# A fused two-block kernel: the opening's norm sums moved to TensorE and its order rewritten

## What is computed

```python
def rms_norm(x, w):
    y = x * lax.rsqrt(jnp.mean(x * x, axis=-1, keepdims=True) + EPS)
    return y * w
def modulate(x, norm_w, shift, scale):
    return rms_norm(x, norm_w) * (1 + scale) + shift

mod_l = silu(c) @ ada_w[0] + ada_b[0]       # six vectors of 1024; the same for ctx with c_ctx
hl = modulate(x,   norm_mix_w[0], sh1,  sc1)
hc = modulate(ctx, norm_mix_w[0], csh1, csc1)
pl, pc = hl @ w_in, hc @ w_in
```

## Time and profile before

| | |
|---|---|
| three executions, median | 2278.91 us (2278.24 to 2280.76) |
| profiled execution, its own time | 2280.79 us |
| its span in the profile | 2278.8 us |
| TensorE busy (matmuls) | 2218.6 us, 97% of the span |
| VectorE, ScalarE, GpSimd busy | 52%, 39%, 41% |
| mean granted clock of TensorE | 0.993 of full |

### The profile page before, as it was taken

One profiled execution on the slowest core, in us unless ns is written; L12 is line 12 of the kernel. 1 busy time (PEld: TensorE's weight loads), 2 busy tenths in 40 slices (PEclk: granted clock), 3 DMA queues, 4 the chain that ended last, 5 costly groups with the idle time before them and its releaser, 6 DMA issues.

```text
span 2278.8 us, 36911 instructions
## 1 busy us (share of the span) xinstructions
PE 2218.6 (97%) x13959; PEld 1904.4 (84%) x13959; DVE 1177.3 (52%) x1926; ACT 879.6 (39%) x1532; POOL 935.8 (41%) x767
## 2 busy tenths in 40 slices
PE   6999999999999999999999999999999999999998
PEld 4878979888888888888899988888888887788777
DVE  5784781657777763335244365553334115762273
ACT  5434343341111113325455442223444236742572
POOL 2435453343343333325343155554665441154313
PEclk9999999999999999999999999999999999999999
DMA  7242241125555541111211025553223232123212
GB/s 281 77 149 75 73 160 61 56 93 194 193 193 189 189 147 59 61 65 65 76 43 33 10 93 190 188 184 120 92 94 107 93 101 75 49 84 94 78 48 74
DMA packets 67720, 245.40 MB, mean 108 GB/s; under 512 B 7376, under 2 KB 11728, under 8 KB 66960
## 3 DMA queue, kind: packets, MB, share of 16 engines
q1 hardware_dynamic: 67360, 242.94, 31.4%
q0 software_dynamic: 240, 0.79, 0.1%
HBM read 240.81 MB, written 2.10 MB: 107 GB/s over the span
## 4 chain that ended last, share of the span: by engine, by line
PE 78%; DVE 7%; issue 7%; POOL 4%; ACT 3%; DMA 0%; POOLq 0%; DVEq 0%; SPq 0%; ACTq 0%
PE ps L887 14%; PE ps L888 14%; PE ps L889 14%; PE ps L1779 4%; PE ps L1781 4%; PE ps L1782 4%; POOL w_low L489 4%; PE ps L924 2%; PE ps L926 2%; PE ps L925 2%; PE ps L2009 2%; PE ps L1995 2%; PE ps L636 2%; PE ps L1947 1%; DVE arena L3005 1%
## 5 line engine op out<-in xcount | busy, mean ns | idle before, releaser
L489 POOL TENSOR_TENSOR w_low<-ring,w_high 128x512 fp32r<-128x512 f32 (+2 forms) x534 | 747.5, 1422 | 1048.1 <-ACT w_high L480 1048.1
L480 ACT ACTIVATE w_high<-ring 128x1024 fp32r<-128x1024 f32 (+2 forms) x267 | 275.1, 1031 | 928.4 <-PE ps L889 620.6
L887 PE MATMUL ps<-h_high,w_high 128*128 128x512 f32 x1040 | 408.7, 393 | 8.4 <-DVE h_low L736 5.5
L888 PE MATMUL ps<-h_low,w_high 128*128 128x512 f32 x1040 | 406.0, 390 | 0.0
L889 PE MATMUL ps<-h_high,w_low 128*128 128x512 f32 x1040 | 405.4, 390 | 0.0
L887 PEld LDWEIGHTS ps<-h_high,w_high 128*128 128x128 f32 x1040 | 195.8, 188 | 55.8 <-DVE h_low L736 6.0
L889 PEld LDWEIGHTS ps<-h_high,w_low 128*128 128x128 f32 x1040 | 195.6, 188 | 41.5
L888 PEld LDWEIGHTS ps<-h_low,w_high 128*128 128x128 f32 x1040 | 195.7, 188 | 37.8
L3240 DVE TENSOR_TENSOR hidden<-arena,hidden 128x1536 fp32r<-128x1536 f32 (+1 forms) x42 | 87.2, 2077 | 193.3 <-ACT hidden L2362 193.3
L1779 PE MATMUL ps<-hidden,w_high 128*128 128x512 f32 (+1 forms) x504 | 178.6, 354 | 0.0
L2907 DVE CUSTOM_DVE_ANT_0 const<-const,arena 128x1024 f32<-128x1024 f32 x96 | 149.0, 1566 | 57.2 <-DMA const<-late_w_dram 57.1
(11 more groups left out here) (553 smaller groups left out, 4766.6 us busy)
## 6 DMA issues: line engine op xcount, KB each, us to landing
const<-late_w_dram SPq DMA_DIRECT2D x112, 512.0 KB, 5.0
ring<-up_dram SPq DMA_DIRECT2D x88, 512.0 KB, 3.2
ring<-down_dram SPq DMA_DIRECT2D x44, 512.0 KB, 3.2
XB<-ada_dram SPq DMA_DIRECT2D x22, 768.0 KB, 5.5
ring<-winE_dram SPq DMA_DIRECT2D x32, 512.0 KB, 3.5
ring<-win_dram SPq DMA_DIRECT2D x20, 512.0 KB, 3.2
ring<-winC_dram SPq DMA_DIRECT2D x20, 512.0 KB, 3.5
arena<-ada_dram SPq DMA_DIRECT2D x10, 768.0 KB, 19.8
```

What stands on the lines that cost most here:

```text
L480: nc.scalar.activation(WH[p][:, 0:L], RAW[p][:, 0:L], ACT.Copy).then_inc(w_hi, 1)
L489: ins = nc.gpsimd.tensor_tensor(WL[p][:, to], RAW[p][:, to], WH[p][:, to].bitcast(F32), ALU.subtract)
L887: nc.tensor.matmul(bank[:, 0:n], wh[:, cols], hi, start=(k == 0), stop=False)
L888: nc.tensor.matmul(bank[:, 0:n], wh[:, cols], lo, start=False, stop=False)
```

## The change

- The load of the latents is cut in two halves of four tiles. The load of the context goes behind both pieces of group 2's `ada_w` (the sixth piece).
- The squares of the opening are no longer added on VectorE: each is written to its own place (in the buffer that later holds the scaled tile), and TensorE sums all eight tiles of a sequence itself, so that `mean` takes 64 passes for the latents and 32 for the context.
- Latents and context have a root, an inverse and a bank each. The context's squares, mean, root and spread move behind latent tile 3.
- TensorE's new order: mean of the latents, group sums 0, spread of the latents, turn 0, group sums 1, turn 1, tile 0, group sums 2, turn 2, tiles 1, 2, 3, mean of the context, group sums 3, spread of the context, turn 3, group sums 4, tile 4, turn 4, group sums 5, tile 5, turn 5, tiles 6 and 7.
- ScalarE's row copies go behind the high parts of the tiles ahead of them; in `hgrn`, `split_hi` of a chunk goes before the wait for the context sums of the same turn instead of behind their exponential.

The core of the diff:

```diff
-    adaT=(FIRST_MODS, (4,)), n0=(3, (1, 5, 6)), ...
+    adaT=(FIRST_MODS, (4,)), n0=(4, (1, 5, 6, 3)), ...
-ADDED = ("n0", "n1", "n3", "n5", "n6")
+ADDED = ("n1", "n3", "n5", "n6")
-BATCHED = dict(n0=(range(2),), ro0=(range(4),), ...
+BATCHED = dict(ro0=(range(4),), ...
         def square_at(stage, k, j):
+            if stage == "n0":
+                return H[k][:, j, :]
...
-            sp.dma_start(XL, dram["xl"]).then_inc(x_first, 16)
-            sp.dma_start(XC, dram["xc"]).then_inc(x_in, 16)
+            for x in range(2):
+                some = slice(KT // 2 * x, KT // 2 * (x + 1))
+                sp.dma_start(XL[:, some, :], dram["xl"][:, some, :]).then_inc(x_first[x], 16)
             for u in range(2 * FIRST_MODS):
...
+                if u == 5:
+                    sp.dma_start(XC, dram["xc"]).then_inc(x_in, 16)
...
+            mean(pe, "n0", 0)
             mod_sums(0)
-            for k in range(2):
-                mean(pe, "n0", k)
+            spread(pe, "n0", 0)
             mod_turn(0)
-            spread(pe, "n0", 0)
             mod_sums(1)
+            mod_turn(1)
+            first_latent(0)
+            mod_sums(2)
+            mod_turn(2)
+            first_latent(1)
+            first_latent(2)
+            first_latent(3)
+            mean(pe, "n0", 1)
+            mod_sums(3)
             spread(pe, "n0", 1)
-            mod_turn(1)
-            mod_sums(2)
-            first_latent(0)
-            mod_turn(2)
-            mod_sums(3)
-            first_latent(1)
             mod_turn(3)
-            first_latent(2)
             mod_sums(4)
-            first_latent(3)
+            first_latent(4)
             mod_turn(4)
-            first_latent(4)
             mod_sums(5)
...
-            for j in range(KT):
-                square("n0", 0, j)
-            act.wait_ge(x_in, 16)
-            for j in range(KT):
-                square("n0", 1, j)
+            for x in range(2):
+                act.wait_ge(x_first[x], 16)
+                for j in range(KT // 2 * x, KT // 2 * (x + 1)):
+                    square("n0", 0, j)
+            root("n0", 0)
             mod_row(0)
             for k in range(2):
                 split_hi("win0", k)
-            root("n0", 0)
+            shift_high("n0", 0, (0,))
             mod_row(1)
-            shift_high("n0", 0, (0,))
+            shift_high("n0", 0, (1,))
             mod_row(2)
-            shift_high("n0", 0, (1,))
+            shift_high("n0", 0, (2,))
+            act.wait_ge(x_in, 16)
+            for j in range(KT // 2):
+                square("n0", 1, j)
+            shift_high("n0", 0, (3,))
+            for j in range(KT // 2, KT):
+                square("n0", 1, j)
+            root("n0", 1)
             mod_row(3)
-            shift_high("n0", 0, (2, 3))
+            shift_high("n0", 0, (4,))
             mod_row(4)
-            shift_high("n0", 0, (4, 5))
+            shift_high("n0", 0, (5,))
             mod_row(5)
...
+                    if i and not (r and c < 2):
+                        split_hi(win, c + 2)
                     bank = await_sums(act, win, g)
                     taken(A(A_b[d][:, j, a:a + n], bank[:, 0:n], ACT.Exp, scale=-1.0), win, g)
-                    if i and not (r and c < 2):
-                        split_hi(win, c + 2)
...
-            for k, j in squared("n0"):
-                if j:
-                    add_square("n0", k, j)
             invert("n0", 0)
             first_columns(0)
...
             scale_tile("n0", 0, 3)
+            invert("n0", 1)
             first_columns(3)
```

More of the change, by code:

```diff
@@ L114 @@
 SUMS = dict(
-    adaT=(FIRST_MODS, (4,)), n0=(3, (1, 5, 6)), win0=(19, B5), hgS0=(6 * SCORE_SUMS, (0, 1, 2, 3)), hgK0=(6 + ROUND_MODS[0], (5,)), hgU0=(12, (4, 6)), ro0=(5, (5, 6)),
+    adaT=(FIRST_MODS, (4,)), n0=(4, (1, 5, 6, 3)), win0=(19, B5), hgS0=(6 * SCORE_SUMS, (0, 1, 2, 3)), hgK0=(6 + ROUND_MODS[0], (5,)), hgU0=(12, (4, 6)), ro0=(5, (5, 6)),
     win1=(19, B5), hgS1=(6 * SCORE_SUMS, (0, 1, 2, 3)), hgK1=(6 + ROUND_MODS[1], (5,)), hgU1=(12, (4, 6)), ro1=(5, (5, 6)),
@@ L156 @@
 NORM_STAGES = [x for x in SUMS if x in ("n0", "ro0", "ro1", "n1", "n2", "nlat", "nqk", "n3", "n4", "n5", "n6")]
-ADDED = ("n0", "n1", "n3", "n5", "n6")
-LAST_APART = ADDED[1:]
+ADDED = ("n1", "n3", "n5", "n6")
 PAIRED = (("n2", 0), ("n4", 0))
-BATCHED = dict(n0=(range(2),), ro0=(range(4),), ro1=(range(4),), nlat=(range(1), range(1, 5)), nqk=(range(9),))
+BATCHED = dict(ro0=(range(4),), ro1=(range(4),), nlat=(range(1), range(1, 5)), nqk=(range(9),))
 RS_COLS = 48
@@ L370, in two_blocks @@
         late_c, late_silu = sem("late_c"), sem("late_silu")
-        x_in, x_first = sem("x_in"), sem("x_first")
+        x_in, x_first = sem("x_in"), [sem(f"x_first{x}") for x in range(2)]
         raw_full, raw_spent, down_spent = ([sem(f"{x}{p}") for p in range(2)] for x in ("raw_full", "raw_spent", "down_spent"))
@@ L506, in squared @@
                 last = 2 if stage == "n6" else 0
-                if stage == "n0":
-                    return [(k, j) for k in range(len(items)) for j in range(KT)]
                 return [(k, j) for j in range(KT - last) for k in range(len(items))]\
@@ L521, in places @@
         def places():
-            return [(x, k, j) for x in NORM_STAGES for k, j in squared(x) if x not in ADDED or j]
+            return [(x, k, j) for x in NORM_STAGES for k, j in squared(x) if x != "n0" and (x not in ADDED or j)]
         def await_square_used(eng, u):
@@ L565, in last_square @@
             last = k == batches(stage)[batch_of(stage, k)][-1] and j == len(ITEMS[stage][k][0]) - 1
-            return last and (stage not in ADDED or stage in LAST_APART)
+            return last
         def item_width(stage, k):
@@ L576, in square_place @@
                 return added(stage, k)
+            if stage == "n0":
+                return square_at(stage, k, j)
             u = square_use(stage, k, j)
@@ L620, in mean @@
             at = column_at(stage, k)
-            tiles_ = [KT - 2, KT - 1] if stage in LAST_APART else [KT - 1] if stage in ADDED else range(1, KT, 2) if (stage, k) in PAIRED else range(len(srcs))
+            tiles_ = [KT - 2, KT - 1] if stage in ADDED else range(1, KT, 2) if (stage, k) in PAIRED else range(len(srcs))
             now = tiles_ if some is None else some
@@ L625, in mean @@
             for j in now:
-                if stage in ADDED and not (stage in LAST_APART and j == KT - 1):
+                if stage in ADDED and j < KT - 1:
                     await_square_used(pe, square_use(stage, k, j))
@@ L640, in mean @@
                     sums_done(ins, *mean_sum(stage, b))
-                elif stage not in ADDED:
+                elif stage not in ADDED and stage != "n0":
                     ins.then_inc(sq_used, 1)
@@ L2156, in _ @@
             load_table(ROOT)
-            act.wait_ge(x_first, 16)
-            for j in range(KT):
-                square("n0", 0, j)
-            act.wait_ge(x_in, 16)
-            for j in range(KT):
-                square("n0", 1, j)
+            for x in range(2):
[3 more added lines that the diff above has]
+            root("n0", 0)
             mod_row(0)
```

## The result

The changed kernel takes **2294.87 us** (median of 4 runs, 2294.57 to 2296.87) against 2279.34 (4 runs, 2278.24 to 2280.76): ratio 1.0064, 95% interval 1.005 to 1.0078. It is slower by 15.5 us, three times what a measurement can tell. The profiled execution took 2295.01 us, with a span of 2292.9.

A forecast was written before the change was run, and what follows sets the result against it. TensorE, 97% busy without slack behind the opening, was taken as the bound. Chunk 2's delay of 15.2 plus 1.5 clock loss, say 16.5 us, gave 2297.3 profiled, less 1.9 for the median: 2295.4 us, range 2288 to 2300.

The forecast's parts named there:

- clock loss: Behind the context's sums, group sums 3, spread and turn 3 run partly at half level: 1.5 us, bounds 0 and 2.8.
- Loads: Opening: the latents' first half lands at 9.1 us instead of 11.60, 2.5 us earlier; the later context load is in time.
- Latents' sums: Opening, TensorE: 64 one-column passes at the lower clock level take 14.6 us and end at 24.3, against 22.91 before.
- the first rival: Full-level sums: unbroken sums wake TensorE, the latents' mean ends at 17.0, chunk 2 is 6.9 late; 2285.8 us, chance 0.07.
- Up to tile 0: Opening, from group sums 0 behind the mean: turn 0 ends at 29.9, tile 0 comes at 35.5, 4.5 us later than before.
- Tiles 1 to 3: Opening, behind tile 0: tile 2 comes at 41.7 and tile 3 at 45.2 us, against 40.16 for tile 3 before.
- the second rival: More waiting: TensorE's longer waits bring another clock fall, 1.5, and the halves land together, 2.5; 2299.4 us or more, chance 0.08.
- Context and group 3: Behind tile 3, called the dearest step: context's sums, group sums 3, spread, turn 3; tile 4 at 56.1, 13.9 us later.
- Tile 7 to chunk 2: End of the opening: the old 10.2 us chain of context tiles, less under half a microsecond; chunk 2 at 75.4.
- To the end: Behind the opening TensorE has no slack, so a shift of chunk 2's start moves the end by as much.
- an absorbed opening: Rival: TensorE later waits on something with its own clock, such as a load, ending the shift; 2279 us, chance 0.05.

The follow-up runs named there:

- the sixth experiment: The changed kernel with all latents in one load and the context's load right behind it: 2298.9 us, ratio 1.0076.
- The fourth: The changed kernel with 128 columns of ones instead of one for the latents' 64 passes: 2288.97 us, ratio 1.0043.
- fifth experiments: The changed kernel with five dense 128x512 matmuls, results unused, on TensorE ahead of the latents' 64 passes: 2290.98 us in one run.
- the first: The changed kernel with group 3 put back ahead (sums 3 before tile 1, turn 3 before tile 2): 2291.6 us, ratio 1.0052.
- the second: The changed kernel with the squares added on VectorE again, leaving TensorE 8 passes for the latents and 4 for the context: 2289.06 us, ratio 1.0039.
- the tenth: The kernel with additions on VectorE and group 3 ahead, plus group 4's sums ahead of tile 3 and turn 4 ahead of tile 4: 2282.34 us, ratio 1.0015.
- the third: The changed kernel with additions back on VectorE and group 3 ahead: 2284.16 us, ratio 1.0014.
- seventh: The changed kernel with additions back on VectorE, the context's split, and a new TensorE order; halves, late context load and two roots kept: 2274.12 us, ratio 0.9958.
- the last two experiments: Additions on VectorE and group 3 ahead, plus either context squares earlier with additions spread (2283.86 us) or group 4's sums ahead of tile 3 (2282.34 us).

## Why the prediction was right

The forecast was 2295.4 in a range of 2288 to 2300, the measurement 2294.87. The mechanism was right in the main: the passes cost what the lower level makes of them, the late tiles push chunk 2 back by 15.9 us, and nearly all of that reaches the end. That the time was met to 0.5 us is in part luck, as the steps show: a clock loss put in the wrong place stood in for one that was missing, and the lag shrank on its way to the end. Step by step:

- **Loads.** First half expected at 9.1, seen at 9.09; what it gains (2.5 expected) was 2.6 at chunk 2 in the sixth experiment.
- **Latents' sums.** 14.6 us at the lower level, end at 24.3; measured 13.78 (0.215 a pass) and 23.64. The fourth and fifth experiments show the reason that was given, not just the size: the 64 unbroken one-column passes stayed at the lower level where they began at it, and fell to it where they began at the upper. The Trainium skill ("TensorE: Matmul & The Clock Gate", Part 1) says that sustained matmul activity brings the full level, and names no exception for narrow matmuls; read so, it would have led towards the first rival. These runs disagree with it for one column (13.78 us) and agree with it for 128 (9.49).
- **Up to tile 0.** Turn 0 to end at 29.9 and tile 0 at 35.5; 29.4 and 35.1. The upper level was taken to come during spread and turn 0; it came only behind group sums 1, which took 2.79 where 1.5 was taken. They, not the high part of tile 0, then set turn 1 (32.86, 0.70 us behind them); it ended at 33.7 where 34.1 was expected, so the error cost nothing.
- **Tiles 1 to 3.** Tile 3 expected at 45.2, came at 46.16. This is the term missing from the sum: the clock fell at about 36, behind a wait of 1.44, and tile 0 (2.4 instead of 1.4) and group sums 2 (2.26 instead of 1.5) ran partly at the lower level.
- **Clock loss.** 1.5 us were put behind the context's sums, as one-column sums were taken to pull the clock down; there was none there, though such a fall came in three of the experiments. So the size was near, the place wrong, and that is luck: the rows showed a fall behind a long wait, and the same had to be asked of the wait ahead of tile 0, which the second rival did with a chance of 0.08 for the whole rival.
- **Context and group 3.** The gap from tile 3 to tile 4 was 10.9 expected and 11.03 measured. But calling this order the dearest step was wrong as a cause: undone alone it gives 1.6 at chunk 2 (3.3 in the time). The gap adds work that has to be done somewhere (sums 3, turn 3, the context's passes); of the whole 15.9, passes and order together give 12.8.
- **Tile 7 to chunk 2.** 9.8 expected, 9.98 measured. Chunk 2 came at 76.09, where the sum without the clock loss had 75.4 and with it 76.9. The terms as listed from tile 2 to tile 7 add up to some 0.6 us less than the instants given with them (the step behind tile 3 to 9.3, not 9.5), so part of this agreement is rounding.
- **To the end.** A late start of chunk 2 was to reach the end whole. Of 15.9 us 14.1 did. In the experiments the shift of the end, span against span, differs from that of chunk 2 by up to 3.6 us: 14.3 became 11.0 in the first, 7.4 became 8.7 in the second, 10.2 became 6.8 in the fourth, 3.6 became 0.0 in the tenth, and nothing changed in the third and seventh. The traces of the changed kernel and of the one before differ behind chunk 2 in where the clock falls; that this is all of it is not shown.

The rivals: full-level sums (2285.8) and an absorbed opening (2279) did not happen; of "more waiting" the extra fall did, ahead of tile 3, but the halves landed apart.

## What to carry to other kernels

Price a sum over partitions on TensorE by its passes and the clock that they leave, not by its columns: 64 one-column passes cost 13.8 us where eight passes behind VectorE's additions cost 1.8 and ended 6 us earlier, and TensorE was the bound while VectorE had nothing else to do. In a hand-written order put ready work into each wait of the bounding engine ahead of the chain's next link; here that, with the halved load kept and the additions back, turned a loss of 0.6% into a gain of 0.4%. And a gap in the timeline is not what closing it gains: ask which of the work in it disappears and which only moves.

## What the runs showed of the hardware that was not expected

- The same 64 sums are faster with 128 columns (9.49 us) than with one (13.78), with the same number of weight loads: the passes came down to the price of the upper level in the one case and not in the other.
- Started at the upper level, unbroken one-column passes lost it some 5 us later (at 18 us, TensorE 100% busy), in one run.
- The opening as a whole started up to 1.1 us earlier in some runs (additions done at 14.8 to 15.9 us with the same code ahead of them; the last two experiments, on another chip than the other eight, have the early ones), so an instant in one profile has to be counted from the sums before it is compared with one in another run.
